# A weight slot shared by the raw chunk and its low part, reloaded after its matmuls

## The chip, the cores and the metric

The kernel runs on one core of a Trainium2 chip. The metric is the device time of one launch in microseconds; lower is better. All times here are in microseconds (us) unless marked ns.

## The reference

A decoder trunk of two layers on a sequence of 256 tokens, model width 2048, everything in float32:

```python
for layer in range(DEPTH):                     # DEPTH = 2
    hn = rmsnorm(h, norm_mix[layer])
    if layer < N_A:                            # layer 0
        h = h + rglru_block(hn, ...)           # in-projection, conv, gated recurrence, out-projection
    else:                                      # layer 1
        h = h + mla_block(hn, k_sh, v_sh, ...) # low-rank queries, causal attention, out-projection
    h = h + swiglu(rmsnorm(h, norm_ffn[layer]), ffn_w_in[layer], ffn_w_out[layer])
    if layer == N_A - 1:
        k_sh, v_sh = shared_kv(h, ...)         # compressed keys and values from the stream
```

The widths are 2048 for the recurrence, 5632 for the SwiGLU feed-forward network (FFN), 16 heads of 128+64 for queries and keys and 128 for values, and 512 for both latents. The weights, 375 MB in all, are read once.

## The kernel before

**Products in three passes.** TensorE multiplies in a reduced float32 format. To keep the precision, each operand is split into a rounded high part and the remainder, its low part: x = hi + lo. Each product takes three matmuls, hi*hi, hi*lo and lo*hi (`products`, L1249, and `lru_tiles`, L1374). The activations are split once per stage (`act_hi`, `act_lo`). The weights are split as they stream in.

**Weight chunks.** The weights come as 360 chunks of usually 128 x 2048 float32 (1 MB: four row tiles of 128 by 512 columns), numbered in the order of use (`C_REC` to `CHUNKS`, L47). Chunk n lives in slot n % 4 of three buffers of four slots each: `raw`, into which the DMA loads it, `w_hi` and `w_lo`. Its way:

1. SyncE issues the load (`load`, L291) once `w_lo_done` says that chunk n-4 has been split.
2. ScalarE writes `w_hi` = rounded `raw` (`split`, L424). It waits for the load (`raw_in`) and for `chunk_used`, which says that the matmuls of chunk n-4 are done.
3. VectorE writes `w_lo` = `raw` - `w_hi` (`split`, L763), once `w_hi_done` is up, and raises `w_lo_done`.
4. TensorE waits for `w_lo_done`, runs the chunk (24 matmuls of 512 columns, or 48 of 256 in the recurrent layer) and raises `chunk_used` (`chunk`, L1262).

**The order on the engines** is written out by hand. Each engine has one queue that it works through in order. While TensorE runs chunk n, ScalarE and VectorE have the split of chunk n+4 in their queues, and between the splits stand the other steps of the stage:

- *Recurrent layer:* 16 chunks of the in-projection with a convolution on VectorE, then 4 gate chunks in 8 blocks (L575 and L1397), whose results ScalarE turns into sigmoids; a block needs the PSUM banks of the block two before it. Then 16 chunks with the recurrence and a GELU beside them (L613, L994).
- *SwiGLU up loop* (`up`, L500, L840, L1335): 11 iterations of 8 chunks, four for the gate half (c = 0 to 3), four for the up half (c = 4 to 7). ScalarE applies the SiLU at c = 3. VectorE multiplies the two halves at c = 7 (L852), in its queue behind the split issued at c = 6, and raises `g_done`. TensorE transposes the product after the first chunk of the next iteration (`transpose_g`, L1326).
- *Down projections* (`down`, L476, L809, L1309): groups of four chunks, one per 512 output columns. In the last group, at b = 0 to 3, VectorE adds the result to the stream (`update`), ScalarE takes the squares for the next norm, TensorE transposes the block before (`transpose_h`) and both helpers write its `act_hi` and `act_lo`; then comes the split of step b.
- *Latent projections:* 8 chunks of w_dkv (128 x 1152, L639) and 4 of w_dq (L672), with norms of both latents.
- *Attention:* 8 head pairs p (`pair`, L687, L1063, L1497), each with a key/value chunk (even number, 128 x 2048) and a query chunk (odd number, loaded as 128 x 1536). On ScalarE the queue of a pair is: exponentials of the pair before, squares of the keys, copies of the transposed keys and queries, split of the even chunk, copy of the transposed probabilities `pT` (L723), squares of the queries (L730), output copy, values copy (L694), split of the odd chunk. TensorE runs the even chunk, the head transposes (after VectorE's `s_max`), the odd chunk, the attention matmuls (L1478, which need `pT`) and the scores.

Both splits take a chunk's size from `chunk_size` (L413) where its number is a Python integer; in a loop over a register they take 2048 columns, so the query splits work on 2048 columns of the slot, of which 1536 are loaded.

```python
def load(m, s, src, dst=None):
    if not (isinstance(m, int) and m == 0):
        sp_.wait_ge(w_lo_done, 4 * m + s - 3)
    sp_.dma_start(raw[:, s, :, :] if dst is None else dst, src).then_inc(raw_in[s], 16)
```

Of the kernel before, what the change touches and what calls it, by code (L numbers as in the profile page):

```python
# [18 lines left out]
F32 = mybir.dt.float32  # L19
# [6 lines left out]
P = 128  # L26
# [5 lines left out]
W = 512  # L32
KC = 4
FB = FF // W
NB = D // W
HEADS, NOPE, ROPE, QK, VD = 16, 128, 64, 192, 128
PAIRS = HEADS // 2
KV_LORA = Q_LORA = 512
DKV = KV_LORA + ROPE
# [13 lines left out]
C_DKV = C_DOWN0 + 4 * FB  # L53
C_DQ = C_DKV + 8
C_PAIR = C_DQ + 4
C_WO = C_PAIR + 2 * PAIRS
# [21 lines left out]
def act_slot(g):  # L78

    return 4 * g if g < 2 else 8 + 4 * (g % 2)  # L80
# [8 lines left out]
def build_program(nc, a, out):  # L89
    x, positions = a["x"], a["positions"]  # L90
    ctx = ExitStack()
    with ctx:
        def sb(name, shape, dt=F32, stack=ctx):
            return stack.enter_context(nc.sbuf_tensor(name, shape, dt))

        def sem(name):
            return ctx.enter_context(nc.semaphore(name))
# [2 lines left out]
        h = sb("h", [P, NT, D])  # L100
        act_hi = sb("act_hi", [P, KT, SEQ], F32R)
        act_lo = sb("act_lo", [P, KT, SEQ], F32R)
        raw = sb("raw", [P, 4, KC, W])
        w_hi = sb("w_hi", [P, 4, KC, W], F32R)
        w_lo = sb("w_lo", [P, 4, KC, W], F32R)
        gtmp = sb("gtmp", [P, NT, W])
        utmp = sb("utmp", [P, 4, 260])
# [65 lines left out]
        w_lo_done = sem("w_lo_done")  # L173
        chunk_used = sem("chunk_used")
# [111 lines left out]
        @block.sync  # L286
        def _(sp_):
            for t in range(NT):
                sp_.dma_start(h[:, t, :], x[0, t * P:(t + 1) * P, :]).then_inc(x_in[t], 16)

            def load(m, s, src, dst=None):  # L291

                if not (isinstance(m, int) and m == 0):
                    sp_.wait_ge(w_lo_done, 4 * m + s - 3)
                sp_.dma_start(raw[:, s, :, :] if dst is None else dst, src).then_inc(raw_in[s], 16)

            def tile_rows(w, r, c, width=W):
                return w[r:r + KC * P, :].rearrange("(k p) n -> p k n", p=P)[:, :, bass.ds(c, width)]

            w_in = a["lru_w_in"][0]  # L300
            for dst, src in vec_loads[:6]:
                sp_.dma_start(dst, src, allow_slow_non_contiguous=True).then_inc(vec_in, 16)
            for s in range(4):
                if s == 1:
                    sp_.wait_ge(vec_in, VEC_ALL)
                load(0, s, tile_rows(w_in, s * KC * P, D))
            with sp_.Fori(1, NB) as j:
                for s in range(4):
                    load(j + C_REC // 4, s, tile_rows(w_in, s * KC * P, j * W + D))
            gate_rows = a["lru_w_gate"][0].rearrange("n d e -> (n d) e")  # L310
            for s in range(4):
                load(C_GATE // 4, s, tile_rows(gate_rows, s * KC * P, 0))
            with sp_.Fori(0, NB) as j:
                for s in range(4):
                    load(j + C_GEL // 4, s, tile_rows(w_in, s * KC * P, j * W))

            def down(w, c0, groups):
                by_group = w.rearrange("(g k p) n -> p g k n", k=KC, p=P)
                with sp_.Fori(0, groups) as g:
                    for b in range(NB):  # L320
                        src = by_group[:, bass.ds(g, 1), :, b * W:(b + 1) * W]
                        load(g + c0 // 4, b, src.rearrange("p g k n -> p (g k) n"))

            def up(w, c0):
                with sp_.Fori(0, FB) as i:
                    for c in range(8):
                        col = i * W + (c // 4) * FF
                        load(2 * i + (c0 // 4 + c // 4), c % 4, tile_rows(w, (c % 4) * KC * P, col))

            down(a["lru_w_out"][0], C_LOUT, 4)  # L330
            up(a["ffn_w_in"][0], C_UP0)
            down(a["ffn_w_out"][0], C_DOWN0, FB)
            for j in range(8):
                src = a["w_dkv"][2 * j * P:(2 * j + 2) * P, :].rearrange("(k p) n -> p k n", p=P)
                dst = raw[:, j % 4, :, :].rearrange("p k n -> p (k n)")[:, 0:2 * DKV]
                load((C_DKV + j) // 4, j % 4, src, dst.rearrange("p (k n) -> p k n", k=2))
            for s in range(4):
                load(C_DQ // 4, s, tile_rows(a["w_dq"][0], s * KC * P, 0))
            w_ukv = a["w_ukv"].rearrange("c h d -> c (h d)")
            w_uq = a["w_uq"][0].rearrange("c h d -> c (h d)")  # L340
            with sp_.Fori(0, PAIRS // 2) as i:
                for u in range(2):
                    load(i + C_PAIR // 4, 2 * u, tile_rows(w_ukv, 0, i * (2 * W) + u * W))
                    dst = raw[:, 2 * u + 1, :, :].rearrange("p k n -> p (k n)")[:, 0:KC * 2 * QK]
                    load(i + C_PAIR // 4, 2 * u + 1, tile_rows(w_uq, 0, i * (4 * QK) + u * 2 * QK, 2 * QK),
                         dst.rearrange("p (k n) -> p k n", k=KC))
            down(a["w_o"][0], C_WO, 4)
            up(a["ffn_w_in"][1], C_UP1)
            down(a["ffn_w_out"][1], C_DOWN1, FB)
            out_v = out[0].rearrange("(t p) d -> p t d", p=P)  # L350
            for b in range(NB):
                sp_.wait_ge(h_done, 3 * NB + b + 1)
                sp_.dma_start(out_v[:, :, b * W:(b + 1) * W], h[:, :, b * W:(b + 1) * W]).then_inc(stored, 16)
            sp_.wait_ge(stored, 16 * NB)
# [56 lines left out]
                eng.wait_ge(gT_dve, g + (f0 + 1))  # L411

        def chunk_size(n):  # L413
            return 2 * DKV if C_DKV <= n < C_DQ else KC * W

        def flat_chunk(buf, s, size):
            return buf[:, s, :, :].rearrange("p k n -> p (k n)")[:, 0:size]
# [3 lines left out]
        def _(act):  # L421
            A = nc.scalar

            def split(m, s):  # L424

                if isinstance(m, int) and 4 * m + s >= CHUNKS:
                    return
                size = chunk_size(4 * m + s) if isinstance(m, int) else KC * W
                act.wait_ge(raw_in[s], 16 * m + 16)
                if not (isinstance(m, int) and m == 0):  # L430
                    act.wait_ge(chunk_used, 4 * m + s - 3)
                A.activation(flat_chunk(w_hi, s, size), flat_chunk(raw, s, size), ACT.Copy).then_inc(w_hi_done, 1)  # L432
# [26 lines left out]
            def stationary(d, g, slot):  # L459

                source_ready(act, d, g)
                if not isinstance(g, int) or g >= 4:
                    act.wait_ge(chunk_used, 4 * g + (DOWN_C[d] - 4))
                elif d == 2:
                    act.wait_ge(chunk_used, DOWN_C[d] - (g == 0))
                else:
                    act.wait_ge(chunk_used, DOWN_C[d] - 3 + g)
                A.activation(act_hi[:, slot:slot + 4, :], feat[:, bass.ds(4 * g, 4), :], ACT.Copy).then_inc(st_hi, 1)  # L468
# [64 lines left out]
            act_tiles("x", 0)  # L533
            act_tiles("x", 1)
            split(0, 0)
            split(0, 1)
            act_tiles("x", 2)
# [75 lines left out]
            for s in range(16):  # L613
                n = C_GEL + s
# [72 lines left out]
            def pair(m, u, live=True, mid=True, old=True, first=False, last=False):  # L687
                p = 2 * m + u

                def values():  # L690

                    act.wait_ge(k_norm, p + 1)
                    for t in range(NT):
                        i = A.activation(v_sb[:, u, t, :, :], kv_psum(t)[:, :, NOPE:NOPE + VD], ACT.Copy)  # L694
                    i.then_inc(v_done, 1)
# [40 lines left out]
                if live:  # L736
                    if not first:
                        values()
                    if last:

                        stationary(2, 0, act_slot(0))
                    split(m + (C_PAIR // 4 + 1), 2 * u + 1)

            pair(0, 0, mid=False, old=False, first=True)
            pair(0, 1, old=False)
            with act.Fori(1, PAIRS // 2 - 1) as m:
                pair(m, 0)
                pair(m, 1)
# [11 lines left out]
        def _(dve):  # L760
            V = nc.vector

            def split(m, s):  # L763

                if isinstance(m, int) and 4 * m + s >= CHUNKS:
                    return
                size = chunk_size(4 * m + s) if isinstance(m, int) else KC * W
                dve.wait_ge(w_hi_done, 4 * m + s + 1)
                V.tensor_tensor(flat_chunk(w_lo, s, size), flat_chunk(raw, s, size),  # L769
                                flat_chunk(w_hi, s, size).bitcast(F32), ALU.subtract).then_inc(w_lo_done, 1)  # L770
# [223 lines left out]
            for s in range(16):  # L994
                n = C_GEL + s
# [67 lines left out]
            def pair(m, u, live=True, mid=True, old=True, last=False):  # L1063
# [37 lines left out]
                if isinstance(m, int) and p == PAIRS:  # L1101
                    split(C_WO // 4, 2)
                if mid:
                    split(m + (C_PAIR // 4 + (u + 1) // 2), (2 * u + 3) % 4)
                if live:

                    dve.wait_ge(k_rs, p + 1)
# [452 lines left out]
```

## Time and profile before

| | |
|---|---|
| three runs | 2078.63, 2078.1, 2080.23 us; median 2078.63 |
| span of the profiled execution | 2076.5 us |
| TensorE matmul (PE) busy | 98% |
| TensorE weight load (PEld) busy | 84% |
| VectorE (DVE) busy | 53% |
| ScalarE (ACT) busy | 44% |
| GpSimd (POOL) busy | 5% |
| read from HBM | 375.08 MB, 182 GB/s over the span |
| load queue q1 | 54.2% of the 16 DMA engines' span |
| granted TensorE clock, mean | 0.999 of full speed |

The span goes from the first to the last instruction on the core. The profile lists no total time of its own for the profiled execution beside this span; the span lies 2.1 us below the median of the runs. PE is the matmul part of TensorE, PEld its weight load; matmuls are pipelined, so that the busy share of PE is not its share of peak. L432 is line 432 of the kernel. An entry such as [3.52 <-PE bank L1256] says that the engine had idled for 3.52 us and which instruction ended that. SPq is the queue from which SyncE issues loads.

### The profile page before, as it was taken

How to read it: one execution, taken by the hardware profiler on the slowest of the kernel's cores; microseconds unless marked ns; L12 is line 12 of the kernel's file. 1: busy time of each engine (PE TensorE's matmuls, PEld its weight loads, DVE VectorE, ACT ScalarE, POOL GpSimd, SP SyncE). 2: the span in 40 equal slices, each digit the busy share in tenths (PEclk: the TensorE clock that was granted, in tenths of full speed). 3: DMA queues.
4: the chain of work that ended last, by engine and by line, in shares of the span. 5: the costliest groups of instructions: out<-in, count | busy, mean ns of one | idle time of the engine just before them, and what ended most of it. 6: DMA issues, size and time to landing. Idle time of an engine off the chain costs nothing. (4 is left out here: it accounts for less than half of the span.)

```text
span 2076.5 us, 25468 instructions
## 1 busy us (share of the span) xinstructions
PE 2035.5 (98%) x10163; PEld 1733.9 (84%) x10163; DVE 1103.5 (53%) x1016; ACT 917.5 (44%) x888; POOL 96.7 (5%) x113
## 2 busy tenths in 40 slices
PE   6999999999999999999999999999999999999999
PEld 6999988888888888888897888888888888888887
DVE  7768545444444444444467885554444444454543
ACT  4468435334333334343465554453433333443432
POOL 3230000000000000000002220000000000000000
PEclk9999999999999999999999999999999999999999
DMA  7554665555555555555544334465565555555552
GB/s 269 182 179 157 212 198 177 193 183 184 198 182 195 189 184 181 202 196 188 176 157 159 107 121 167 166 204 193 182 201 183 189 186 190 183 202 185 199 188 95
DMA packets 190153, 377.94 MB, mean 182 GB/s; under 512 B 6122, under 2 KB 10484, under 8 KB 189716
## 3 DMA queue, kind: packets, MB, share of 16 engines
q1 hardware_dynamic: 189576, 375.98, 54.2%
q0 software_dynamic: 272, 1.13, 0.2%
q8 instruction: 37, 0.61, 0.1%
q10 hardware_dynamic: 252, 0.09, 0.0%
q14 instruction: 16, 0.13, 0.0%
HBM read 375.08 MB, written 2.10 MB: 182 GB/s over the span
## 5 line engine op out<-in xcount | busy, mean ns | idle before, releaser
L769 DVE TENSOR_TENSOR w_lo<-raw,w_hi 128x2048 fp32r<-128x2048 f32 (+1 forms) x360 | 818.9, 2277 | 772.3 <-ACT w_hi L432 771.8
L432 ACT ACTIVATE w_hi<-raw 128x2048 fp32r<-128x2048 f32 (+1 forms) x360 | 683.1, 1900 | 796.0 <-PE bank L1256 739.4
L1256 PE MATMUL bank<-w_hi,act_hi 128*128 128x512 f32 (+2 forms) x2592 | 1005.4, 388 | 3.5 <-DVE act_lo L774 1.3
L1256 PE MATMUL bank<-w_hi,act_lo 128*128 128x512 f32 (+2 forms) x2592 | 999.9, 386 | 0.0
L1256 PE MATMUL bank<-w_lo,act_hi 128*128 128x512 f32 (+2 forms) x2592 | 998.9, 385 | 0.0
L1256 PEld LDWEIGHTS bank<-w_hi,act_hi 128*128 128x128 f32 x2592 | 486.7, 188 | 99.4 <-issue 2.0
L1256 PEld LDWEIGHTS bank<-w_hi,act_lo 128*128 128x128 f32 x2592 | 486.5, 188 | 96.9
L1256 PEld LDWEIGHTS bank<-w_lo,act_hi 128*128 128x128 f32 x2592 | 486.8, 188 | 95.1
L1381 PE MATMUL bank<-act_hi,w_hi 128*128 128x256 f32 x512 | 145.7, 285 | 5.0 <-DVE w_lo L769 5.0
L1381 PE MATMUL bank<-act_hi,w_lo 128*128 128x256 f32 x512 | 145.6, 284 | 0.0
L1381 PE MATMUL bank<-act_lo,w_hi 128*128 128x256 f32 x512 | 145.6, 284 | 0.0
L1381 PEld LDWEIGHTS bank<-act_hi,w_hi 128*128 128x128 f32 x512 | 99.1, 193 | 5.2 <-issue 5.2
L1381 PEld LDWEIGHTS bank<-act_lo,w_hi 128*128 128x128 f32 x512 | 99.0, 193 | 0.0
L1381 PEld LDWEIGHTS bank<-act_hi,w_lo 128*128 128x128 f32 x512 | 99.0, 193 | 0.0
L514 ACT ACTIVATE gtmp<-bank,stats 128x512 f32<-128x512 f32 x44 | 27.9, 686 | 74.7 <-PE bank L1256 74.7
L473 ACT ACTIVATE feat_all<-bank 128x512 f32 (+1 forms) x22 | 13.1, 597 | 97.7 <-PE bank L1331 97.7
L1187 POOL TENSOR_SCALAR stats<-stats 128x2 f32<-128x2 f32 (+1 forms) x7 | 5.3, 753 | 1069.5 <-DVE stats L837 1029.5
L852 DVE SCALAR_TENSOR_TENSOR gtmp<-bank,stats,gtmp 128x512 f32<-128x512 f32 x44 | 31.0, 747 | 27.7 <-PE bank L1256 27.7
L774 DVE SCALAR_TENSOR_TENSOR act_lo<-bank,cols,act_hi 128x256 fp32r<-128x256 f32 x72 | 30.2, 476 | 24.2 <-ACT act_hi L442 14.5
L800 DVE TENSOR_TENSOR act_lo<-feat_all,act_hi 128x1024 fp32r<-128x1024 f32 x30 | 36.6, 1219 | 8.9 <-ACT act_hi L468 8.9
L806 DVE COPY feat_all<-bank 128x512 f32 (+1 forms) x22 | 15.2, 691 | 47.1 <-PE bank L1331 47.1
L455 ACT ACTIVATE utmp<-h 128x512 f32<-128x512 f32 x24 | 14.9, 624 | 44.0 <-DVE h L794 44.0
(166 smaller groups left out, 781.4 us busy)
## 6 DMA issues: line engine op xcount, KB each, us to landing
raw<-in_ffn_w_in SPq DMA_DIRECT2D x176, 1024.0 KB, 5.0
raw<-in_ffn_w_out SPq DMA_DIRECT2D x88, 1024.0 KB, 5.0
raw<-in_lru_w_in SPq DMA_DIRECT2D x32, 1024.0 KB, 5.5
raw<-in_lru_w_out SPq DMA_DIRECT2D x16, 1024.0 KB, 5.0
raw<-in_w_o SPq DMA_DIRECT2D x16, 1024.0 KB, 5.0
raw<-in_w_ukv SPq DMA_DIRECT2D x8, 1024.0 KB, 5.6
raw<-in_w_uq SPq DMA_DIRECT2D x8, 768.0 KB, 4.7
raw<-in_w_dkv SPq DMA_DIRECT2D x8, 576.0 KB, 3.8
```

Of the source, the lines that this page charges most:

```text
L432: A.activation(flat_chunk(w_hi, s, size), flat_chunk(raw, s, size), ACT.Copy).then_inc(w_hi_done, 1)
L455: i = A.activation(junk[:, t, :], h[:, t, b * W:(b + 1) * W], ACT.Square, accum_out=stat(SS_D + NB * t + b))
L473: A.activation(feat[:, bass.ds(4 * i, 2), :], ps[4][:, :].rearrange("p (a b) -> p a b", a=2), ACT.Copy).then_inc(gT_act, 1)
L514: k = A.activation(gtmp[:, t, :], ps[t][:, :], ACT.Silu, scale=stat(RS + 2 * (d + 1) + t))
L769: V.tensor_tensor(flat_chunk(w_lo, s, size), flat_chunk(raw, s, size), flat_chunk(w_hi, s, size).bitcast(F32), ALU.subtract).then_inc(w_lo ...
L774: return V.scalar_tensor_tensor(out=act_lo[:, k, :], in0=src, scalar=g, in1=act_hi[:, k, :].bitcast(F32), op0=ALU.mult, op1=ALU.subtract)
L800: V.tensor_tensor(act_lo[:, slot:slot + 4, :], feat[:, bass.ds(4 * g, 4), :], act_hi[:, slot:slot + 4, :].bitcast(F32), ALU.subtract).then ...
L806: V.tensor_copy(feat[:, bass.ds(4 * i + 2, 2), :], ps[5][:, :].rearrange("p (a b) -> p a b", a=2)).then_inc(gT_dve, 1)
L852: k = V.scalar_tensor_tensor(out=gtmp[:, t, :], in0=ps[2 + t][:, :], scalar=stat(RS + 2 * (d + 1) + t), in1=gtmp[:, t, :], op0=ALU.mult, o ...
L1187: step(G.tensor_scalar(stat(rs, n), stat(ss, n), 1.0 / width, EPS, ALU.mult, ALU.add))
L1256: i = T.matmul(outs[t], x_part, wp, start=first and n == 0, stop=last and n == 2)
L1381: i = T.matmul(lru_bank(idx, q), w_part, x_part, start=first and kk == kks[0] and n == 0, stop=last and kk == kks[-1] and n == 2)
```

## The change

`raw` gets the address of `w_lo`: the name is taken and given back before `w_lo` is allocated, so both cover the same bytes. VectorE's subtraction thus reads the raw chunk and writes the low part over it. As the matmuls read `w_lo`, a slot can be reloaded only after them: the load of chunk n waits for `chunk_used` of chunk n-4 instead of `w_lo_done`. ScalarE's and VectorE's waits stay as they are. No instruction changes its place in any queue.

The second part concerns sizes. `chunk_size` returns 1536 for the query chunks (odd numbers from `C_PAIR` to `C_WO`), and the splits in the attention loops ask it with `of_pair=True`. The query splits on both engines work on 1536 columns instead of 2048.

```diff
         act_lo = sb("act_lo", [P, KT, SEQ], F32R)
-        raw = sb("raw", [P, 4, KC, W])
         w_hi = sb("w_hi", [P, 4, KC, W], F32R)
+
+        with nc.sbuf_tensor("raw", [P, 4, KC, W], F32) as raw:
+            pass
         w_lo = sb("w_lo", [P, 4, KC, W], F32R)
...
             def load(m, s, src, dst=None):
 
                 if not (isinstance(m, int) and m == 0):
-                    sp_.wait_ge(w_lo_done, 4 * m + s - 3)
+                    sp_.wait_ge(chunk_used, 4 * m + s - 3)
...
         def chunk_size(n):
-            return 2 * DKV if C_DKV <= n < C_DQ else KC * W
+            if C_DKV <= n < C_DQ:
+                return 2 * DKV
+            return KC * 2 * QK if C_PAIR <= n < C_WO and n % 2 else KC * W
...
-            def split(m, s):
+            def split(m, s, of_pair=False):
...
-                size = chunk_size(4 * m + s) if isinstance(m, int) else KC * W
+                size = chunk_size(4 * m + s if isinstance(m, int) else s + (C_PAIR if of_pair else 0))
...
-                    split(m + (C_PAIR // 4 + 1), 2 * u + 1)
+                    split(m + (C_PAIR // 4 + 1), 2 * u + 1, True)
...
-                    split(m + (C_PAIR // 4 + (u + 1) // 2), (2 * u + 3) % 4)
+                    split(m + (C_PAIR // 4 + (u + 1) // 2), (2 * u + 3) % 4, True)
```

The change of `split` stands twice in the kernel, once for ScalarE and once for VectorE; the two calls are ScalarE's and VectorE's for the query chunk.

## Rows read from the trace of the kernel before

**Rows 1.** The page's costliest groups: line engine op, shapes xcount, busy us, mean ns, idle before.
```profile
L769 DVE TENSOR_TENSOR w_lo<-raw,w_hi 128x2048 fp32r<-128x2048 f32 (+1 forms) x360 | 818.9, 2277 | 772.3 <-ACT w_hi L432 771.8
L432 ACT ACTIVATE w_hi<-raw 128x2048 fp32r<-128x2048 f32 (+1 forms) x360 | 683.1, 1900 | 796.0 <-PE bank L1256 739.4
```

**Rows 2.** The page's DMA issues: KB of each, median us from issue to landing.
```profile
raw<-in_ffn_w_in SPq DMA_DIRECT2D x176, 1024.0 KB, 5.0
...
raw<-in_lru_w_in SPq DMA_DIRECT2D x32, 1024.0 KB, 5.5
...
raw<-in_w_ukv SPq DMA_DIRECT2D x8, 1024.0 KB, 5.6
```

**Rows 3.** Timelines of an FFN up iteration: start us, us, engine, instruction, idle before.
```profile
716.97 1.92 ACT L432 ACTIVATE w_hi<-raw 128x2048 fp32r<-128x2048 f32 x1 [3.52 <-PE bank L1256]
722.41 1.92 ACT L432 ACTIVATE w_hi<-raw 128x2048 fp32r<-128x2048 f32 x1 [3.52 <-PE bank L1256]
...
724.36 2.29 DVE L769 TENSOR_TENSOR w_lo<-raw,w_hi 128x2048 fp32r<-128x2048 f32 x1 [3.15 <-ACT w_hi L432]
727.94 1.41 DVE L852 SCALAR_TENSOR_TENSOR gtmp<-bank,stats,gtmp 128x512 f32<-128x512 f32 x2 [1.29 <-PE bank L1256]
...
726.82 0.37 SPq L295 DMA_DIRECT2D raw<-in_ffn_w_in  x1
...
732.87 1.03 PEld L1331 LDWEIGHTS bank<-ident,gtmp 128*128 128x128 f32 x8
```

**Rows 4.** Timelines of the gate blocks in the recurrent layer, ScalarE and TensorE.
```profile
121.19 1.94 ACT L432 ACTIVATE w_hi<-raw 128x2048 fp32r<-128x2048 f32 x1
...
136.44 1.93 ACT L432 ACTIVATE w_hi<-raw 128x2048 fp32r<-128x2048 f32 x1
...
141.09 1.99 ACT L432 ACTIVATE w_hi<-raw 128x2048 fp32r<-128x2048 f32 x1
143.01 0.84 ACT L583 ACTIVATE feat_all<-bank,cols 128x256 f32<-128x256 f32 x2
...
126.05 0.50 PE L1381 MATMUL bank<-rec_split,w_hi 128*128 128x256 f32 x2 [0.69 <-ACT gtmp L583]
...
139.87 0.39 PE L1381 MATMUL bank<-rec_split,w_hi 128*128 128x256 f32 x1 [0.70 <-ACT gtmp L583]
```

**Rows 5.** Timelines of the last group before the first FFN, VectorE and TensorE.
```profile
315.44 1.28 DVE L794 TENSOR_TENSOR h<-h,bank 128x512 f32<-128x512 f32 x2
...
323.58 1.28 DVE L794 TENSOR_TENSOR h<-h,bank 128x512 f32<-128x512 f32 x2
...
342.14 1.65 DVE L774 SCALAR_TENSOR_TENSOR act_lo<-bank,cols,act_hi 128x256 fp32r<-128x256 f32 x4
...
326.71 1.04 PE L1277 MATMUL bank<-ident,h 128*128 128x128 f32 x8
```

**Rows 6.** Timelines of the latent stage's end: query squares, first head transposes.
```profile
1109.87 0.69 ACT L682 ACTIVATE utmp<-bank,stats 128x512 f32<-128x512 f32 x1 [2.10 <-PE bank L1256]
...
1130.09 0.33 PE L1454 MATMUL bank<-ident,kn 128*128 128x128 f32 x1 [2.70 <-DVE qr L1137]
```

**Rows 7.** Timelines of one head pair, TensorE and ScalarE.
```profile
1162.59 0.39 PE L1256 MATMUL bank<-w_hi,act_lo 128*128 128x512 f32 x1
...
1170.32 0.59 PE L1478 MATMUL bank<-pT,v_sb 128*128 128x256 f32 x2
...
1179.50 0.39 PE L1256 MATMUL bank<-w_hi,act_lo 128*128 128x512 f32 x1
...
1168.48 0.48 ACT L723 ACTIVATE pT<-bank 128x384 f32<-128x384 f32 x1
```

**Rows 8.** Groups of instructions on VectorE: line, op, shapes xcount, busy us, mean ns.
```profile
L1137 DVE TENSOR_TENSOR qr<-qr,rot 128x256 f32<-128x256 f32 x8 | 3.4, 425 | 0.3
...
L1110 DVE TENSOR_TENSOR kn<-bank,stats 128x256 f32<-128x256 f32 x16 | 6.7, 418 | 3.1 <-POOL stats L1240 3.1
```

**Rows 9.** Stretch at the start: window, length, busy us (instructions) per engine, PEclk, DMA, GB/s.
```profile
25.80:29.40 3.60, 3.57 (x18) 3.60 (x19) 3.60 (x6) 3.60 (x6) 0.00 (x0) 0.56 0.67 177
```

More of the change, by code:

```diff
@@ L761, in _, with split @@
             V = nc.vector
-            def split(m, s):
+            def split(m, s, of_pair=False):
                 if isinstance(m, int) and 4 * m + s >= CHUNKS:
                     return
-                size = chunk_size(4 * m + s) if isinstance(m, int) else KC * W
+                size = chunk_size(4 * m + s if isinstance(m, int) else s + (C_PAIR if of_pair else 0))
                 dve.wait_ge(w_hi_done, 4 * m + s + 1)
```

## The prediction

> **What bounds the kernel now.** I read the engine shares first: TensorE is busy in nearly the whole span, so anything that delays it counts. The costliest groups come next [rows 1]: VectorE's weight subtraction (360 times 2.28 us) idles mainly for ScalarE, and ScalarE's rounding pass (1.90 us) idles mainly for TensorE, so both helpers wait for slots and not the other way round. The DMA list gives the time from issue to landing of a chunk [rows 2]. Then the timelines, for what releases what: in the SwiGLU up loop ScalarE starts the split of a chunk when its slot's old matmuls end (722.41), VectorE follows at 724.36, ends at 726.65, and only then is the next load of the raw slot issued, 0.17 later (726.82) [rows 3]. The same place one chunk earlier starts ScalarE at 716.97, so a chunk of 24 matmuls is 5.44 us. The load is a whole chunk ahead of its user: at the issue of 726.82 its ScalarE pass is some 12 us away. This is the lead that the change spends.
>
> **The new chain.** After a chunk's last matmul at U: issue U+0.17 (as after VectorE's end), landing L later, ScalarE 0.05 after it (as fast as VectorE follows ScalarE, 0.03), then 1.92, 0.03 and 2.29 [rows 3]. With L=5.0 [rows 2] the chunk is ready at U+9.5; before it was at U+4.3. TensorE has three other chunks, 16.3 us, in the meantime: in plain stretches 6.8 us of cover are left and the cost is nothing. Bandwidth is no issue either: one load per 5.44 us, as before. But both engines take their queues in order. ScalarE now stands in a split until U+7.1 instead of U+1.9, VectorE until U+9.5 instead of U+4.3, and whatever is queued behind a split starts up to 5.2 us later. So I look for what stands behind a split and is awaited by TensorE.
>
> **Part 1, the gate transpose.** In each up block VectorE multiplies the gate (two instructions, 1.41 us) behind the split that follows column chunk 6. It started at 727.94, and TensorE takes the result with a weight load at 732.87 [rows 3]. Now: U of chunk 6 is 722.37; issue 722.54, landing 727.54, ScalarE to 729.5, VectorE to 731.8, product to 733.2. TensorE gets it at 733.25 instead of 732.87: 0.4 us, 11 times per FFN, 22 times: **+8.8 us** (ends: L of 4.8 gives 0.2 and 4.4 us, 5.3 gives 0.7 and 15).
>
> **Part 2, the LRU gates.** ScalarE's sigmoids empty the banks that TensorE needs two blocks later, with splits between them. The split at 121.19 [rows 4] must now wait for a load issued after 119.7; with L=5.5 [rows 2] it starts at 125.4, 4.3 late, and block 2 starts at 130.35 instead of 126.05. The split of 136.44 would come at 140.7, but its slot is freed at 136.2 and lands at 141.9: 5.5 late. The split of 141.09 would come at 146.6, its slot is freed at 143.4 and lands at 149.1: 8.0 late, and with it the sigmoid of 143.01. That one had 1.0 us to spare before the next projection (two blocks of 2.87 after 139.87 make 145.6; the sigmoids end at 144.5): **+7.0 us** (5 to 8.5). In the GELU part behind it both helpers are full and 5.7 us later as a whole; the two longest VectorE runs, before the split of the fourth and the eighth chunk, had about 5 us to spare: **+1.0** (0 to 2).
>
> **Part 3, entries of the two FFNs (d=0 and 2).** In the last group before them VectorE's residual update stands behind a split, so the run of updates, squares and rounding starts 4.0 us late. It repeats every 8.14 us (315.44 to 323.58) against TensorE's 6.4 (a chunk's 5.44 and eight transposes, as at 326.71) [rows 5], and so never catches up. The third update ended at 324.86, 1.6 us before TensorE's weight load for the transpose (326.5); now it ends at 328.8. The four steps cost 0.3, 0.35, 1.75 and, at the last activation tile (ended at 343.8 with 0.7 to spare), 0.8: 3.2 each, **+6.4** (4 to 9).
>
> **Part 4, from the second FFN into attention (d=1).** The updates are again 4.0 late, 0.4 of it absorbed, so the first latent chunk, which needs their second activation tile, starts 3.5 later: +3.5. The first w_dq chunk is loaded after latent chunk 4: 0.17+5.0+0.05+4.2, and the overlapping load, make 10.0 against three chunks of 3.16: +0.5. At 1109.87 ScalarE squares the query latent as soon as the last w_dq chunk is done [rows 6]; now both helpers stand in a split whose load (L=5.6) starts with the chunk before, ready 10.0 after it, where the squares' data come 6.2 after it: +3.4 with the rest of the chain to the transpose. Last, the split of the third pair's values chunk stands before the values copy and the query squares: 5.8+1.9+0.7 = 8.4 after the first pair's chunk against 5.6: +2.8. The transposes of 1130.09 come **10.2 us** late (7 to 13).
>
> **Part 5, the pairs.** Period 16.91 (1162.59 to 1179.50 [rows 7]). On ScalarE the probability copy of 1168.48 stands behind the even split. New loop: even chunk done at U=1162.98, +0.17, L=5.3 to 5.6, +0.05, 1.80 to the copy, 0.49, 0.15 to TensorE's attention matmul: 1170.95, where it was 1170.32, then 9.58 to the next U: period 17.5 to 17.9. Five pairs stretch by 0.6 (the one before has 2 us of idle time to absorb it): **+3.2** (1 to 5). The query splits get shorter by a quarter, 0.57 us on VectorE and 0.48 on ScalarE, eight times; they lie beside the longer loop, so I count nothing (at most 4.6 back, if VectorE stayed the loop's limit).
>
> **Part 6, writing in place.** No row shows the subtraction over its own input. The nearest are an addition over its input, 425 ns for 256 columns, and a multiplication to another tile, 418 [rows 8]: nothing, since VectorE's splits are mostly covered; a tenth more (0.23) in the chains above would add 22x0.23, some 5 us.
>
> **Sum:** 8.8+7.0+1.0+6.4+10.2+3.2 = 36.6 us. Against the profiled execution: span 2076.5 to 2113.1. The median of the runs lies 2.1 above that span, so the time is **2115.2 us**.
>
> One price has another value in the notes. The rows give 5.0 us from issue to landing for 1 MB [rows 2]. The Trainium skill (DMA: Bandwidth & Descriptors, section Bandwidth) has 6.15 us of transfer alone for 1 MB (issued from GpSimd). Taking it as an estimate, 1.15 more per load, each of the 22 stalls grows by 1.15 and the sum would be about 80 us, 2159. The trace disagrees, and I stay with its rows.
>
> **Rivals.**
> (a) *All of it is hidden.* Three chunks of cover, and the landing usually far from needed. For it: 6.8 us to spare in plain stretches. Against: the queue positions in parts 1 to 5, each of which needs only 0.4 to 4 us. Time 2076 to 2081. Chance 0.05.
> (b) *The pairs get faster and nothing else slower.* The attention stretch is the one place where VectorE's queue sets the period, and its query split shrinks by 0.57 us: if the loads hide, eight pairs give 4.6 us back, 2074.0. It decides where L plus ScalarE's pass stays under 7.3 us after the even chunk; the rows give 7.9. Chance 0.03.
> (c) *Loads land later at their new place*, now that each starts just as matmuls, ScalarE and VectorE all turn to new slots: rows of lone loads go up to 5.7, 0.7 more than I took. By the 22 stalls (+15) and the longer chains (+10) the time is about 2140. Against: most loads of a kind agree within 0.3. Chance 0.10.
> (d) *TensorE's clock falls in the new gaps.* After 5.0 us without matmuls at the start the granted clock was 0.56 for 3.6 us, partly at the 1.2 GHz level, 1.6 us lost [rows 9]. The forecast has three gaps of 3.5 to 4.3 us; all three would cost 4.8: 2120. The gap of 2.7 us before 1130.09 [rows 6] left no trace in the clock. Chance 0.12. The Trainium skill (TensorE: Matmul & The Clock Gate, section on HAM oscillation) says that an idle stretch throttles the array again; by it (d) is as likely as the gaps are long.
>
> **How the numbers follow.** Forecast 0.70, (c) 0.10, (d) 0.12, (a) 0.05, (b) 0.03. The low ends of the parts add to 4.4+5+0+4+7+1 = 21.4 us, 2100; the high ends to 52.5, 2131, and they will not all meet. The range 2100 to 2132 leaves out (a), (b) and most of (c). About 0.2%, 4.2 us, is what a measurement of this kernel can tell from no change. Slower is everything but (a) and (b): 0.92; same 0.05; faster 0.03.
>
> **What would show it.** In the new profile: ScalarE's splits released by the DMA and no longer by TensorE; 22 waits of 0.2 to 0.7 us of TensorE for the gate product; a gap of 4 to 5 us near 126 us; a period of 17.5 us or more in the pairs; VectorE's splits still 2.28 us, eight ScalarE and VectorE splits a quarter shorter. Wrong would be: TensorE still released everywhere as before (a), or a landing over 5.5 us for FFN chunks (c), or a PEclk slice under 9 (d).

## The result and the profile after

| | before | after |
|---|---|---|
| median of the runs | 2079.43 (2078.1 to 2080.81, 4 runs) | 2113.61 (2112.41 to 2113.74, 4 runs) |
| profiled execution | span 2076.5, clock 0.999 | span 2111.8, clock 0.993 |

The ratio is 1.0163, 95% interval 1.0151 to 1.0175: the change makes the kernel 34 us slower. The forecast was 2115.2, range 2100 to 2132. The spans differ by 35.3 us where the sum of the parts had 36.6.

The page of the changed kernel, busy shares and TensorE's granted clock by 40 slices (the third is under 9, which the forecast had named as the sign of rival (d)), then the two groups that answer to [rows 1]:

```profile
span 2111.8 us, 25468 instructions
...
PE 2051.9 (97%) x10163; PEld 1740.3 (82%) x10163; DVE 1095.3 (52%) x1016; ACT 916.0 (43%) x888; POOL 90.4 (4%) x113
...
PEclk9989999999999999999999999999999999999999
...
L773 DVE TENSOR_TENSOR w_lo<-raw,w_hi 128x2048 fp32r<-128x2048 f32 (+1 forms) x360 | 814.9, 2266 | 905.2 <-ACT w_hi L436 904.7
L436 ACT ACTIVATE w_hi<-raw 128x2048 fp32r<-128x2048 f32 (+1 forms) x360 | 679.9, 1891 | 1061.4 <-DMA raw<-in_ffn_w_in 545.3
```

ScalarE's rounding pass used to be released by TensorE; now the DMA does it. It sits idle 1061 us instead of 796. TensorE's share fell by one point only, and what it lost is spread over some thirty places. The waits view of the same kernel (who waits, on what, us in total, times, longest) names them:

```profile
PEld bank L1335 <- DVE gtmp L856: 9.0, 22, 0.7
PEld bank L1482 <- ACT pT L727: 8.4, 5, 2.1
PEld bank L1385 <- ACT gtmp L587: 7.9, 2, 4.3
PEld bank L1260 <- DVE act_lo L778: 6.4, 4, 3.6
```

In that order: the gate product (22 times, Part 1), the probability copy of five pairs (Part 5), the sigmoids of the gate blocks (Part 2) and the activation tiles (Parts 3 and 4).

To see what each wait is worth, I laid the two traces side by side: for each of TensorE's stages, its start after minus its start before. The growth of this shift across a stage is what the stage lost.

| stage | shift at its start, at its end | lost | forecast |
|---|---|---|---|
| start and in-projection | 0, 0.8 | 0.8 | 0 |
| gate blocks (Part 2) | 0.8, 10.5 | 9.7 | 7.0 |
| GELU part (Part 2) | 10.5, 11.4 | 0.9 | 1.0 |
| into FFN d=0 (Part 3) | 11.4, 14.6 | 3.2 | 3.2 |
| its up loop (Part 1) | 14.6, 16.8 | 2.2 | 4.4 |
| latent stage into attention (Part 4) | 16.8, 28.1 | 11.3 | 10.2 |
| pairs (Part 5) | 28.1, 30.4 | 2.3 | 3.2 |
| into FFN d=2 (Part 3) | 30.4, 33.4 | 3.0 | 3.2 |
| its up loop (Part 1) | 33.4, 35.4 | 2.0 | 4.4 |

Two parts are off by more than 2 us, in opposite directions: the gate blocks and the gate product. Both gaps of the gate blocks are in TensorE's timeline:

```profile
130.52 0.80 PE L1385 MATMUL bank<-rec_split,w_hi 128*128 128x256 f32 x2 [4.14 <-ACT gtmp L587]
...
147.97 0.80 PE L1385 MATMUL bank<-rec_split,w_hi 128*128 128x256 f32 x2 [3.35 <-ACT gtmp L587]
```

The first was forecast for 130.35. What follows them is in the windows view (window and its length, then busy us with instructions of PE, PEld, DVE, ACT and POOL, granted clock, DMA share, GB/s):

```profile
130.50:135.00 4.50, 4.48 (x21) 4.48 (x22) 4.32 (x4) 4.26 (x7) 4.46 (x2) 0.50 0.13 48
...
147.90:152.00 4.10, 4.03 (x19) 4.03 (x20) 1.06 (x2) 3.38 (x6) 3.17 (x2) 0.50 0.36 137
152.00:156.00 4.00, 4.00 (x30) 4.00 (x30) 2.12 (x1) 1.57 (x4) 0.86 (x1) 0.83 0.00 0
...
1138.00:1142.00 4.00, 4.00 (x14) 3.09 (x12) 2.73 (x5) 1.56 (x4) 0.00 (x0) 0.50 0.00 0
```

After the gaps the granted clock is 0.50, the 1.2 GHz level, with 19 to 21 matmul records in each of the first two windows. Behind the two gaps of the gate blocks it stays there for some 5.5 us: the windows from 130.50 to 136.50 and from 147.90 to 153.50 have 0.51. In the trace of before, 126 to 132 us has 1.00. This is rival (d), come true beside the forecast and not instead of it. The Trainium skill (TensorE: Matmul & The Clock Gate, section on HAM oscillation) says that idling throttles the array again, and here the trace agrees, though not after every gap: a gap of 3.33 us that ended at 1079.82 left the window of 1080 to 1084 at 1.00.

### The profile page after: what moved, and what is told of

The parts are those of the page before. It is cut to its first block, busy times and chain, and to the rows that moved or that the text cites. A ratio compares the mean times of both kernels' runs of the same rounds, so it can differ in the third digit from the quotient of the medians.

```text
span 2111.8 us, 25468 instructions
## 1 busy us (share of the span) xinstructions
PE 2051.9 (97%) x10163; PEld 1740.3 (82%) x10163; DVE 1095.3 (52%) x1016; ACT 916.0 (43%) x888; POOL 90.4 (4%) x113
## 4 chain that ended last, share of the span: by engine, by line
PE 40%; issue 3%; DMA 2%; ACT 2%; DVE 2%; POOL 1%; DVEq 0%; POOLq 0%; SPq 0%; ACTq 0%
PE bank L1260 38%; ACT w_hi L436 1%; DVE w_lo L773 1%; DMA raw<-in_w_o 1%; PE bank L1335 1%; DMA raw<-in_ffn_w_in 0%; POOL stats L1240 0%; PE bank L1482 0%; PE bank L1497 0%; PE bank L1498 0%; ACT act_hi L446 0%; DMA raw<-in_w_ukv 0%; DVE h L798 0%; DMA raw<-in_w_dq 0%; POOL stats L1244 0%
## 5 line engine op out<-in xcount | busy, mean ns | idle before, releaser
L1385 PE MATMUL bank<-rec_split,w_hi 128*128 128x256 f32 x128 | 27.9, 319 | 7.5 <-ACT gtmp L587 7.5
L472 ACT ACTIVATE act_hi<-feat_all 128x1024 fp32r (+1 forms) x30 | 31.3, 1044 | 0.0
L1385 PEld LDWEIGHTS bank<-rec_split,w_hi 128*128 128x128 f32 x128 | 23.7, 227 | 8.1 <-ACT gtmp L587 7.9
```

The source lines that it names most:

```text
L1385: i = T.matmul(lru_bank(idx, q), w_part, x_part, start=first and kk == kks[0] and n == 0, stop=last and kk == kks[-1] and n == 2)
```

## The experiments

Twelve runs, each against the kernel before on the same chip. "Trace" is TensorE's shift at the end of the program against the trace of before.

| kernel | median us | ratio, 95% interval | trace |
|---|---|---|---|
| changed kernel | 2113.61 | 1.0163 (1.0151 to 1.0175) | +35.4 |
| the same again | 2112.64 | 1.0162 (1.0148 to 1.0175) | +34.4 |
| late wait alone | 2110.02 | 1.0152 (1.0138 to 1.0166) | +31.3 |
| sizes alone | 2075.24 | 0.9983 (0.9974 to 0.9992) | -1.2 |
| late in the recurrent part alone | 2087.81 | 1.0041 (1.0025 to 1.0056) | +10.3 |
| late in attention alone | 2089.72 | 1.0051 (1.0035 to 1.0066) | +11.3 |
| late in the FFNs alone | 2091.69 | 1.0061 (1.0044 to 1.0078) | +12.4 |
| product first | 2107.47 | 1.0134 (1.0117 to 1.015) | +31.9 |
| sigmoids first | 2104.78 | 1.0125 (1.0109 to 1.0142) | +26.4 |
| pair's copies first | 2099.93 | 1.0098 (1.0081 to 1.0115) | +25.5 |
| updates first | 2100.72 | 1.0105 (1.009 to 1.012) | +21.8 |
| all of them first | 2084.74 | 1.0026 (1.0016 to 1.0037) | +7.6 |
| all first, old wait | 2076.93 | 0.999 (0.9981 to 0.9999) | -0.2 |

My theory was that of the prediction: neither bandwidth nor the writing in place costs anything; what costs is what stands behind a split in ScalarE's and VectorE's queues. The rivals stand with the runs.

**1. The two halves of the change.** The late wait alone keeps `raw` in a buffer of its own and the splits at their old sizes:

```diff
-                    sp_.wait_ge(w_lo_done, 4 * m + s - 3)
+                    sp_.wait_ge(chunk_used, 4 * m + s - 3)
```

> Raw chunk and low part keep buffers of their own and the query splits keep 2048 columns; only the load's wait is moved to the end of the old matmuls. Theory (the waits are the whole cost): the time of the changed kernel, 2113.6 us, up to 1 us more. Rival (the subtraction over its own input, or the moved addresses, make a part of it): at least 4 us away from 2113.6.

It is 31.4 us slower than its own runs of before: nearly the whole loss, without any writing in place. The rest is 2.3 us by the ratios, whose intervals overlap; 3.6 us by the medians. Sizes alone has the changed `chunk_size` and calls of `split`, with the old wait and buffer:

> Only the shorter query splits (1536 columns), buffers and waits as in the kernel before. Theory (they lie beside a longer chain): within 1 us of the kernel before, 2079.4. Rival (VectorE's queue sets the pairs' period): 0.57 us in each of eight pairs, 2074.8.

It was expected to change nothing and is 3.3 us faster than its runs of before. TensorE's timeline shows the head transposes of three pairs, two periods:

```profile
1164.91 0.33 PE L1456 MATMUL bank<-ident,kn 128*128 128x128 f32 x1 [0.47 <-DVE stats L1078]
...
1181.43 0.33 PE L1456 MATMUL bank<-ident,kn 128*128 128x128 f32 x1 [0.56 <-DVE stats L1078]
...
1197.84 0.33 PE L1456 MATMUL bank<-ident,kn 128*128 128x128 f32 x1 [0.45 <-DVE stats L1078]
```

The period is 16.5 and 16.4 us, where it was 16.91 [rows 7]: 0.5 per pair, from 1.48 to -1.16 of shift over five pairs. TensorE still waits for VectorE's `stats` there, so VectorE's queue does set the period, and the 1536-column subtraction (1749 ns instead of 2300, below) shortens it. ScalarE's query split is shorter as well (1.50 us instead of 1.93 in this pair), but ScalarE then idles for 3.94 us until VectorE's `stats` release its exponentials, so the gain is VectorE's. That is the mechanism of rival (b). The forecast counted nothing for it.

**2. One stage late at a time**, on the kernel before. The load takes its wait from a flag that is set in one stage only:

```diff
+                    sp_.wait_ge(chunk_used if late[0] else w_lo_done, 4 * m + s - 3)
...
+            late[0] = True
             down(a["lru_w_out"][0], C_LOUT, 4)
```

(here the FFNs; the flag is off again for the loads of the latent and attention stages.)

> Separate buffers; only the loads of the recurrent layer (36 of 360 chunks) wait for the old matmuls. Queue theory with the clock drop that the changed kernel shows after its gap at 126 us: +11 us, 2090.5. Queue theory with the clock drop free: +8, 2087.4. Rival (late loads disturb the running matmuls, so each late chunk costs the same, 34.2/360): +3.4, 2082.9.

> Separate buffers; only the loads of the latent projections and the head pairs (28 chunks) wait for the old matmuls. Queue theory: 1.1 at the first latent chunk (its updates still start on time), 0.5, 3.4, 0.8 and 3.4 up to the first head transposes, some 2 in the pairs: +11.4, 2090.8. Rival (a cost per late chunk): +2.7, 2082.1.

> Separate buffers; only the loads of the four down projections and the two up projections (296 of 360 chunks) wait for the old matmuls. Queue theory: 3.3 at each FFN entry, 22 waits of 0.2 for the gate product, 3.5 at the first latent chunk, about 1 in the last pairs: +15.5, 2095. Rival (a cost per late chunk): +28.1, 2107.5.

The losses by the medians are 9.2, 11.1 and 12.7 us, together 33.0, against 31.4 for the late wait everywhere. The stages add, so each can be judged alone. In the recurrent part the trace rises from 0.65 at the gate blocks to 10.4 behind them, as with the full change. The FFN kernel rises by 2.9 at each entry, by 4.2 in the latent stage (whose updates belong to its late stretch), and by 0.4 and 0.1 us in its two up loops. Part 1 is nearly absent from it.

**3. What stands behind a split, moved ahead of it.** Four kernels keep the whole change, the late wait and writing in place included, and only let other work go first. In the up loop VectorE takes the product before the split of c = 6:

```diff
                             k.then_inc(g_done, 1)
+                            split(2 * i + ((c0 + 10) // 4), 2)
-                        split(2 * i + ((c0 + c + 4) // 4), c % 4)
+                        if c != 6:
+                            split(2 * i + ((c0 + c + 4) // 4), c % 4)
```

> The changed kernel, with VectorE's gate product queued ahead of the split that stood before it. Theory (the split's queue position holds the product back): the 22 waits of TensorE for the product vanish, 4.3 us less, 2109.3. Rival (TensorE would lose it elsewhere, or the split behind is now late for its own matmuls): no change, 2113.6.

TensorE's waits for the gate product are gone from the waits view; VectorE waits for TensorE instead:

```profile
DVE gtmp L856 <- PE bank L1262: 33.7, 22, 1.8
```

The two up loops add about -0.1 and -0.2 us to the shift instead of +2.2 and +2.0, so Part 1 was worth 4.2 of the 6.1 that the median gained.

In the gate blocks ScalarE takes the first sigmoid pair of a chunk before the split:

```diff
-                split((C_GATE + c + 4) // 4, c)
+                    if n == 0:
+                        split(C_GATE // 4, 3)
+                    elif n % 2 == 0:
+                        split((C_GATE + c + 3) // 4, c - 1)
+            split((C_GATE + 7) // 4, 3)
```

> The changed kernel, with ScalarE's sigmoids of the recurrent layer queued ahead of the splits whose loads are still under way. Theory with the clock drop counted: gaps of 4.1 and 3.35 us vanish and the clock stays up, 11 us less, 2102.6. Theory without a price for the clock: 7 to 8 less, 2106. Rival (the sigmoids are late for another reason): no change.

The shift behind the gate blocks is 3.4 instead of 10.5, and the median is 8.8 us lower, where 11 was expected with the clock and 7 to 8 without. One gap is left, two blocks behind the first one, and the granted clock falls there too (0.50 from 135.8 to 139.2):

```profile
136.30 0.58 PE L1390 MATMUL bank<-rec_split,w_hi 128*128 128x256 f32 x1 [3.35 <-ACT gtmp L588]
```

In the pairs the copy of the probabilities goes before the even split, and in the first pair the values copy and query squares too:

```diff
-                if live:
-                    split(m + (C_PAIR // 4 + 1), 2 * u)
                 if old:
                     act.wait_ge(pt_mm, p - 1)
                     A.activation(pT[:, 0, :], ps[7][:, 0:3 * P], ACT.Copy).then_inc(pt_act, 1)
+                if live and not first:
+                    split(m + (C_PAIR // 4 + 1), 2 * u)
...
                     i.then_inc(q_sq, 1)
+                    if first:
+                        split(m + (C_PAIR // 4 + 1), 2 * u)
```

> The changed kernel, with ScalarE's probability copy queued ahead of the even split in every pair, and in the first pair the values copy and the query squares too. Theory: waits for the copy (5 times 1 to 1.8 us, 2.3 net) and the 3.4 before the first head transposes vanish, 6 us less, 2107.6. Rival (the pairs are bound by VectorE's chain, and the waits only fill its slack): 3.4 less at most, 2110.2.

It gained 13.7 us by the medians, more than expected. (The trace gained 9.9; its execution took 2103.72.) The chunk before the first head transposes starts 23.8 late and the transposes 23.25, where the changed kernel had 24.7 and 28.1: the last step of Part 4 is gone. Then each pair gets shorter, as in sizes alone, down to 21.6 at those of the eighth pair, where the changed kernel goes up to 30.4. ScalarE's timeline shows the copy waiting for TensorE only:

```profile
1191.92 0.49 ACT L725 ACTIVATE pT<-bank 128x384 f32<-128x384 f32 x1 [1.64 <-PE bank L1476]
1192.53 1.92 ACT L436 ACTIVATE w_hi<-raw 128x2048 fp32r<-128x2048 f32 x1
...
1208.56 0.49 ACT L725 ACTIVATE pT<-bank 128x384 f32<-128x384 f32 x1 [1.64 <-PE bank L1476]
1208.98 1.92 ACT L436 ACTIVATE w_hi<-raw 128x2048 fp32r<-128x2048 f32 x1
```

So the 0.5 us per pair and the late copy work against each other in the changed kernel. The same place in its own trace:

```profile
1196.15 1.92 ACT L436 ACTIVATE w_hi<-raw 128x2048 fp32r<-128x2048 f32 x1 [2.33 <-DMA raw<-in_w_ukv]
1197.98 0.47 ACT L727 ACTIVATE pT<-bank 128x384 f32<-128x384 f32 x1
...
1214.04 1.91 ACT L436 ACTIVATE w_hi<-raw 128x2048 fp32r<-128x2048 f32 x1 [3.12 <-DMA raw<-in_w_ukv]
1215.86 0.47 ACT L727 ACTIVATE pT<-bank 128x384 f32<-128x384 f32 x1
```

The split is released by the load, the copy starts when it ends, and the period is 17.88 here (17.5 to 17.9 was forecast).

In the last groups before a norm, both helpers take a block's residual update, squares and tiles before the split of the step before:

```diff
                                 act_tiles(d, b - 1)
-                        split(g + (DOWN_C[d] // 4 + 1), b)
+                                split(g + (DOWN_C[d] // 4 + 1), b - 1)
+                            if b == NB - 1:
+                                split(g + (DOWN_C[d] // 4 + 1), b)
+                        else:
+                            split(g + (DOWN_C[d] // 4 + 1), b)
```

> The changed kernel, with each split of the last down group queued behind the next residual update. Theory: the updates start on time, 3.3 less at each FFN entry and 3.4 at the first latent chunk, 10 us less, 2103.6. Rival (the run of updates is bound by its own length, so that its start does not matter): no change.

The trace loses nothing at the FFN entries (9.9 before and 10.0 behind the first) and nothing at the first latent chunk, three steps that cost 3.2, 3.3 and 3.0. All four together, with the same done for the query latent's squares:

> The changed kernel with all four reorderings and, in the latent stage, the query squares and norm ahead of the split before them. Queue theory: 4.3+11+6+10+3.4 less, 2079; within 3 us of the kernel before, with a quarter of the weight buffers saved. Rival (late loads cost something everywhere): stays over 2090.

29 of the 34 us come back with the late wait and the shared buffer (one of three weight buffers saved, a third) still in place. It is 5.9 us slower than its runs of before, where under 3 was expected. What is left in the trace is 1.7 us at the gate blocks' start (the other kernels' traces have 0.3 to 1.8 there), 2.8 within them (a gap of 3.38 us as in the sigmoids' kernel), 1.8 in the latent chunks and 2.9 before the first head transposes; the pairs then give back 1.9.

**4. A version that beats both?** The same order with the old wait and a buffer of its own, and the shorter query splits:

> The same reorderings with raw buffers of their own, early loads and the shorter query splits. Theory: of the waits that the kernel before already has (2.5 us in the gate blocks, 1.3 in the latent stage, some 1 us per pair) it removes the first two, 2075.5. Rival (the order of before was right for early loads): 2079.4 or slower.

It is 1.9 us faster than its runs of before, against 3.3 for sizes alone; the intervals of the two overlap, so no gain by the new order is shown. In the latent stage the moved work delays splits and what stands behind them, as TensorE's timeline shows:

```profile
1067.42 0.37 PE L1280 MATMUL bank<-w_hi,act_hi 128*128 128x288 f32 x1 [1.49 <-DVE w_lo L784]
...
1118.80 0.45 PE L1280 MATMUL bank<-w_hi,act_hi 128*128 128x384 f32 x1 [2.88 <-DVE act_lo L789]
```

In the kernel before there was no idle time at the first place and 1.29 us at the second. This trace loses 2.0 us from there to the first head transposes. About as much more, up to a shift of 2.7 in the pairs, comes with a granted clock of 0.57 in the windows of 1131 to 1135 and 1148 to 1152. The version to keep is the old wait with the shorter query splits, 2075.24 us.

**5. The changed kernel again.** By now the late wait alone stood 3.6 us below the changed kernel, and nothing explained it.

> This is the changed kernel once more, unaltered. Open is why the kernel with the late wait but raw in a buffer of its own ran 3.6 us below the changed one. In the up loops of the changed kernel's trace a 1 MB chunk landed 5.0 us after its issue, in the other traces 4.8. Theory (the loads' landing, not the writing in place): if the chunks land after 4.8 us here too, TensorE's 22 waits for the gate product get shorter by 0.2 us each and the weight loads can take up most of what is left; the up loops then add 0 to 0.1 us per iteration instead of 0.2, and the time is 2110 to 2111.5, within 1.5 us of the kernel with the separate buffer. Rival (writing in place costs): the landing is 4.8 and the time is 2113 to 2114 all the same. If the landing is 5.0 here, both give 2113.6 and the question stays open.

The landing was 5.0 us again, which by the words above leaves the question open for this run. Three readings beside it do not. The subtraction of 2048 columns by shapes, of the changed kernel:

```profile
L773 DVE TENSOR_TENSOR w_lo<-raw,w_hi 128x2048 fp32r<-128x2048 f32 x344 | 790.1, 2299 | 901.9 <-ACT w_hi L436 901.7
...
L773 DVE TENSOR_TENSOR w_lo<-raw,w_hi 128x1536 fp32r<-128x1536 f32 x8 | 14.0, 1749 | 0.0
```

and of the late wait alone, with a buffer of its own:

```profile
L769 DVE TENSOR_TENSOR w_lo<-raw,w_hi 128x2048 fp32r<-128x2048 f32 x352 | 809.5, 2302 | 896.2 <-ACT w_hi L432 895.9
```

2299 ns in place, 2302 not: Part 6 is nothing, as forecast. Second, three kernels that write in place but whose FFN chunks landed after 4.8 us (sigmoids, pair's copies and updates first) delay the gate product by 0.5, 1.0 and 0.9 us in all 22 places. The two traces of the changed kernel, at 5.0 us, have 3.3 and 2.9; the late wait alone, at 4.8, has 0.4. (This is the start of the transposes less the start of the matmul before, less the usual 0.23.) The lists of DMA issues of the first up loop (400 to 1040 us), of the changed kernel:

```profile
raw<-in_ffn_w_in SPq DMA_DIRECT2D x74, 1024.0 KB, 5.0
```

and of the late wait alone:

```profile
raw<-in_ffn_w_in SPq DMA_DIRECT2D x74, 1024.0 KB, 4.8
```

So most of that difference goes with the landing and not with the address; some 0.4 us of it could be the address's or chance. Third, the gate blocks. In this trace they cost 7.0 us instead of 9.7, and the windows view says why:

```profile
126.10:130.50 4.40, 0.46 (x2) 0.46 (x3) 4.40 (x11) 4.37 (x8) 0.43 (x1) 0.77 0.70 219
130.50:135.00 4.50, 4.50 (x23) 4.50 (x23) 4.45 (x4) 3.78 (x7) 4.50 (x2) 0.50 0.05 19
144.60:147.90 3.30, 0.80 (x6) 0.80 (x7) 2.28 (x1) 3.30 (x8) 0.77 (x1) 1.00 0.83 241
147.90:152.00 4.10, 4.10 (x38) 4.10 (x37) 0.65 (x2) 3.20 (x6) 2.42 (x2) 1.00 0.17 65
```

The first gap is followed by 0.50 as before; the second, 3.23 us long, is not. From before it to behind it the shift grows by 2.4 us here and by 4.9 in the first trace of the same kernel. The difference of 2.6 goes with the clock. So does the scatter of the times: of the five runs, from 2109.29 to 2116.02 us, the two slowest have mean granted clocks of 0.991 and 0.992 and the two fastest 0.995.

## Why the prediction was right, by its steps

- **The new chain and Part 2** held. Block 2 started at 130.52 (130.35 forecast); 0.8 of that is the shift that this trace already had at its start, so that its own delay is 3.7 us, where 4.3 was forecast. Without the clock's dip behind the second gap (the repeat's trace) the gate blocks cost 7.0 us, forecast 7.0, and the GELU part 0.8, forecast 1.0. The dip of rival (d) added 2.6 to 2.7. Behind the first gap it cost nothing in the end: the shift peaked at 7.1 and fell back to 5.4, since TensorE waited 0.7 us there already before the change [rows 4].
- **Part 1** had the right place and half the size, 4.2 us instead of 8.8. Timelines of the changed kernel, with the chain of one product from the load's issue to the transposes:

```profile
693.86 0.37 SPq L297 DMA_DIRECT2D raw<-in_ffn_w_in  x1
...
698.92 1.92 ACT L436 ACTIVATE w_hi<-raw 128x2048 fp32r<-128x2048 f32 x1 [3.35 <-DMA raw<-in_ffn_w_in]
...
700.87 2.29 DVE L773 TENSOR_TENSOR w_lo<-raw,w_hi 128x2048 fp32r<-128x2048 f32 x1 [2.98 <-ACT w_hi L436]
703.08 1.40 DVE L856 SCALAR_TENSOR_TENSOR gtmp<-bank,stats,gtmp 128x512 f32<-128x512 f32 x2
...
704.19 0.39 PE L1260 MATMUL bank<-w_hi,act_lo 128*128 128x512 f32 x1
704.53 0.86 PEld L1335 LDWEIGHTS bank<-ident,gtmp 128*128 128x128 f32 x8 [0.38 <-DVE gtmp L856]
704.54 1.09 PE L1335 MATMUL bank<-ident,gtmp 128*128 128x128 f32 x8
```

  The chain is as forecast. From the issue to the weight load there are 10.67 us (10.71 forecast). The last matmul of the chunk starts at 704.19, and an undisturbed weight load would start with it, 10.33 us after the issue, just as in the forecast (732.87 - 722.54). So the weight load is 0.34 us late here, and the waits view has 9.0 us for all 22, 0.41 each, where 0.38 was forecast. What failed is the step from there to TensorE's loss: the forecast counted all of the weight load's delay. In the trace of before, the weight load ran ahead of the transposes that use it:

```profile
732.87 0.40 PE L1256 MATMUL bank<-w_hi,act_lo 128*128 128x512 f32 x1
733.10 1.04 PE L1331 MATMUL bank<-ident,gtmp 128*128 128x128 f32 x8
```

  The load began at 732.87 [rows 3] and the transposes at 733.10, so the first 0.23 us of delay cost nothing. In the changed kernel the transposes start 0.12 us late in this iteration (704.54 instead of 704.42), 0.15 on average, which over 22 is 3.3 us; that they take 1.09 instead of 1.04 adds about 1. The FFNs-alone kernel, whose transposes come only 0.2 us late in all, still shows in the waits view:

```profile
PEld bank L1336 <- DVE gtmp L857: 5.4, 22, 0.3
```

- **Part 3** held: the steps before FFN d=0 were 0.3, 1.7 and 1.2 against 0.3 + 0.35, 1.75 and 0.8, in all 3.2 and, at d=2, 3.0, for 3.2 each. The largest, in TensorE's timeline, with the residual update (`h`) as its releaser:

```profile
340.23 1.09 PE L1281 MATMUL bank<-ident,h 128*128 128x128 f32 x8 [1.58 <-DVE h L798]
```

- **Part 4** lost 3.3 (3.5 forecast), 0.4 (0.5), 3.4 + 0.8 (3.4) and 3.4 (2.8). The 0.8 is the clock again: the eight transposes at 1137.67 take 1.97 us, and the window behind them is at 0.50. In the last step there was a fourth dip, 0.50 from 1150.2 to 1153.5 behind a gap of 3.07 us. TensorE then still waited 0.72 us for the helpers before the head transposes, so the dip did not set their start directly; whether it has a share in the step was not tested.
- **Part 5** had the copy right, periods of 17.9 falling to 17.2, and one item wrong: the shorter query splits, counted at nothing, give 0.5 us per pair wherever the copy is not late, in the first two pairs above all (shift 28.1 to 27.0). Net 2.3 instead of 3.2.
- **Part 6** held, 2299 ns against 2302. The landing held too: 5.0 us from issue to landing, as in [rows 2]. By the longer figure of the Trainium skill (DMA: Bandwidth & Descriptors, section Bandwidth), 6.15 us for 1 MB issued from GpSimd, an estimate of the time would have been about 2159; the trace disagrees with it here.
- **Rivals.** (a) fell: every stage on its own is slower by 9 us or more. (b)'s mechanism exists, but its condition, that the loads hide, fails with the late wait; the sizes alone show it. (c) fell: 5.0 us, as before. (d) happened in part, about 3.5 us of 4.8. Its three gaps became five, of 3.07 to 4.14 us, and the clock fell behind four of them; two of these falls cost time, one none, and one is open.

The total came out within 1.6 us because errors cancelled. Part 1 was 4.6 us too high; against it stand the clock's 3.5 and the 0.8 before the gates that no part has and that varies from trace to trace (0.3 to 1.8); Part 4's last step (0.6 too low) and Part 5 (0.9 too high) nearly make up for each other. The places were right, and undoing them one by one confirms them. The closeness of the sum is luck; that it lies in the range is not.

## What to carry to other kernels

A buffer that is freed later costs little in bandwidth; it costs what is queued behind the instruction that now waits for the load. So list, stage by stage, what stands behind it on its engine and who waits for that; moving such work ahead of the wait gave back 29 of 34 us here, and the same moves showed no gain where the loads were early. Count a wait by how far TensorE's matmuls shift, not by the weight load's idle time: here 0.23 us of each such wait cost nothing.

## What the runs showed that I had not expected

- The clock does not fall after every gap. In one trace it went to 0.50 after gaps of 4.14, 3.35, 3.22 and 3.07 us and not after one of 3.33; in another trace of the same kernel, not after 3.23 us at the same place. Nor does it take a gap of 3 us: the forecast took the gap of 2.7 us before the first head transposes, full speed behind it, as evidence against (d), but in the trace of sizes alone the same gap (2.72 us, ended at 1130.84) is followed by a granted clock of 0.57 in the window of 1130.5 to 1134.5, and 0.8 us are lost.
- The landing of a 1 MB load differs between traces: a median of 5.0 us in the first up loop of before and of both traces of the changed kernel, 4.8 or 4.9 in all the others. It is not the kernel, since others with the same loads have 4.8; the others ran on three chips, the repeat on a fourth, so the chip may be the reason, but no kernel was traced with both landings. With a chain that is 0.15 us too long, 0.2 us decides.
- Cutting a split by a quarter in the pairs, 4.6 us at most by my count, gave 3.3 although VectorE is 53% busy over the span.
